# Routed experts: rows gathered for four pairs of experts at a time from two float32r parts, shared down product at the end of the loop

## The reference

```python
x = layer_norm(DEEPNORM_ALPHA * x + mix, ln1_g[l], ln1_b[l])
top_idx, top_w = route(xf, w_router, router_bias)          # 8 of 64 experts for a token
y = routed_experts(xf, top_idx, top_w, w_gate, w_up, w_down) + swiglu(xf, ws_gate, ws_up, ws_down)
x = layer_norm(DEEPNORM_ALPHA * x + y, ln2_g[l], ln2_b[l])

def swiglu(x, wg, wu, wd):
    return (jax.nn.silu(x @ wg) * (x @ wu)) @ wd            # wg, wu: 1024 x 256, wd: 256 x 1024
```

## Time and profile before

| | us |
|---|---|
| median of 3 runs | 1208.05 |
| lowest, highest | 1207.52, 1208.32 |
| the profiled execution | 1209.04 |
| its span, first to last instruction | 1207.1 |

### The profile page before, as it was taken

The page is one execution under the profiler, slowest core; times in us unless marked ns, Lnnn a source line. Parts: engine busy times, 40 slices in busy tenths (PEclk is TensorE's granted clock), DMA queues, the critical chain, the costliest instruction groups (busy, mean ns, idle before and its releaser), DMA issues.

```text
span 1207.1 us, 17937 instructions
## 1 busy us (share of the span) xinstructions
PE 1175.1 (97%) x7776; PEld 552.7 (46%) x7776; DVE 347.1 (29%) x1057; ACT 262.2 (22%) x513; POOL 10.4 (1%) x20
## 2 busy tenths in 40 slices
PE   7999999999999999999899999999999999999994
PEld 6774544444444444343386655344444444444331
DVE  0434712222222222222243345222222222222224
ACT  1132312212222122221112323122212222122210
POOL 0000000000000000000000000000000000000001
PEclk9999999999999999999999999999999999999998
DMA  9973579999999999999997626799999999999993
GB/s 385 423 301 116 212 301 428 428 426 427 427 426 428 428 426 428 428 427 426 422 397 307 235 100 232 329 427 428 426 426 428 426 427 429 424 427 428 426 428 128
DMA packets 36070, 452.41 MB, mean 375 GB/s; under 512 B 3984, under 2 KB 4112, under 8 KB 6928
## 3 DMA queue, kind: packets, MB, share of 16 engines
q1 hardware_dynamic: 35984, 451.18, 89.1%
HBM read 450.12 MB, written 1.05 MB: 374 GB/s over the span
## 4 chain that ended last, share of the span: by engine, by line
PE 82%; DMA 13%; DVE 3%; issue 1%; POOL 0%; ACT 0%; POOLq 0%; DVEq 0%
PE bank L635 31%; PE bank L669 15%; DMA slots<-in_w_gu 13%; PE bank L537 7%; PE bank L568 5%; PE bank L812 5%; PE bank L740 5%; PE bank L749 2%; PE bank L652 1%; PE bank L759 1%; PE bank L769 1%; PE bank L591 1%; PE bank L845 1%; PE bank L556 1%; PE bank L695 1%; PE bank L699 1%
## 5 line engine op out<-in xcount | busy, mean ns | idle before, releaser
L669 PE MATMUL bank<-slots,low 128*32 128x512 f32 x2048 | 233.0, 595 | 1.1 <-issue 1.1
L635 PE MATMUL bank<-slots,low 128*64 128x512 f32 x1024 | 227.0, 594 | 4.5 <-DMA slots<-in_w_gu 4.5
L635 PE MATMUL bank<-slots,xT 128*64 128x512 f32 x1024 | 226.9, 594 | 1.9 <-DMA slots<-in_w_gu 1.9
L1275 DVE SCALAR_TENSOR_TENSOR yparts<-bank,small,yparts 128x512 fp32r<-128x512 f32 x128 | 96.1, 751 | 271.0 <-ACT yparts L972 271.0
L972 ACT ACTIVATE yparts<-bank,small 128x512 fp32r<-128x512 f32 x128 | 88.0, 688 | 255.6 <-PE bank L669 255.6
L635 PEld LDWEIGHTS bank<-slots,low 128*64 128x64 f32 x1024 | 69.1, 137 | 135.2 <-issue 126.3
L635 PEld LDWEIGHTS bank<-slots,xT 128*64 128x64 f32 x1024 | 68.9, 137 | 132.5 <-issue 127.0
L669 PEld LDWEIGHTS bank<-slots,low 128*32 128x32 f32 x2048 | 60.4, 109 | 138.8 <-issue 138.8
L1267 DVE TENSOR_TENSOR high<-high,bank 128x256 f32<-128x256 f32 x64 | 27.0, 421 | 331.7 <-ACT high L1000 331.7
L537 PEld LDWEIGHTS bank<-high,low 128*128 128x128 bf16 x1536 | 100.0, 147 | 48.7 <-issue 48.7
L1000 ACT ACTIVATE high<-bank 128x256 f32<-128x256 f32 x64 | 24.7, 386 | 417.4 <-PE bank L635 417.4
(11 more groups left out here) (125 smaller groups left out, 662.1 us busy)
## 6 DMA issues: line engine op xcount, KB each, us to landing
slots<-in_w_gu SPq DMA_DIRECT2D x128, 2048.0 KB, 24.6
slots<-in_w_dn SPq DMA_DIRECT2D x64, 2048.0 KB, 24.1
slots<-in_dense SPq DMA_DIRECT2D x30, 1024.0 KB, 15.0
slots<-in_first SPq DMA_DIRECT2D x4, 768.0 KB, 7.9
r<-in_pool_mat SPq DMA_DIRECT2D x2, 1024.0 KB, 24.3
r<-in_ln_g SPq DMA_DIRECT2D x4, 512.0 KB, 4.4
r<-in_ln_b SPq DMA_DIRECT2D x4, 512.0 KB, 5.8
sdn<-in_shared_dn SPq DMA_DIRECT2D x2, 1024.0 KB, 9.7
```

Source lines behind the costliest of these rows:

```text
L635: m = pe.matmul(H[64 * a:64 * a + 64, :], xg[B % 2][:, k, j, a, :], GU[g][:, a, :, k, :], start=k == 0, stop=k == KD - 1)
L669: m = pe.matmul(Y[half][r0:r0 + 32, :], hT[:, kc * P + 64 * a + 32 * t:kc * P + 64 * a + 32 * t + 32], DN[g][:, a, kc, half * 512:(half + ...
L1275: dve.scalar_tensor_tensor(ysp[:, 1, half * 512:(half + 1) * 512], Y[half][:, :], wslot[:, b:b + 1], ysp[:, 0, half * 512:(half + 1) * 512 ...
```

## The change

- x is split into two float32r parts, the rounded x and what is left (`split`, `split_low`), in place of three bf16 parts.
- A block is four pairs (`SPAN = 4`, 256 places). `gather` fills one bank with one channel group k for four pairs: two tiles by two parts, four matmuls of 256 columns. For block 0 it uses banks of which `FIRST_BANKS` says the order.
- The gathered rows have one buffer, 32 cells over the places of `xT` and what follows it. A pair's 8 cells (one for each k) are those that the same pair of the next block's turn writes again, so a gather goes into cells that were just used; `cell` permutes the numbers from block to block.
- `sel` stands once in float32r (for gathering, one buffer) and once in bf16 (`selb`, two buffers, for `turn_sel`). DVE builds both.
- `shared_down` moves from pair 0 to behind pairs 27 to 30, a quarter each, and adds to the accumulators; the first `combine`, in pair 1, starts them. `shared_turn` of tile 1 moves from ahead of pair 0 into it.
- Space: `hT`, `w3` and `selb` now stand in `r8`, so norm 2's rows go into slot 1, when pair 31 is done with its first half. At the end of layer 0 SP waits for pair 31's H ahead of memory and chunk 0, and norm 2's rows come between their halves.

```diff
+SPAN = 4
+BLOCKS = PAIRS // SPAN
+FIRST_BANKS = (4, 5, 6, 7, 2, 1, 6, 7)
...
-            def norms(l, g_, b_):
-                sp.dma_start(lng, g_.rearrange("l (o d) -> l o d", o=1)[l].to_broadcast([P, D])).then_inc(ln_in, 16)
-                sp.dma_start(lnb, b_.rearrange("l (o d) -> l o d", o=1)[l].to_broadcast([P, D])).then_inc(ln_in, 16)
+            def norms(l, i):
+                for to, w in ((lng[i], (ln1_g, ln2_g)[i]), (lnb[i], (ln1_b, ln2_b)[i])):
+                    sp.dma_start(to, w.rearrange("l (o d) -> l o d", o=1)[l].to_broadcast([P, D])).then_inc(ln_in, 16)
+
+            def last_norms(l):
+
+                sp.wait_ge(main.h_half, (l + 1) * PAIRS)
+                norms(l, 1)
...
                 if l:
-                    sp.wait_ge(main.h_full, last + 1)
+                    sp.wait_ge(main.h_full, l * PAIRS)
...
                     sp.dma_start(r[:, a:z], dense[l, 0][:, a:z]).then_inc(chunk_in[0][h], 16)
+                    if h == 0:
+                        last_norms(l - 1)
...
-                sp.wait_ge(*x_at(l, 0, NT - 1))
-                norms(l, ln2_g, ln2_b)
...
+            def gather(ps, k, to):
+
+                for t in range(NT):
+                    for s in range(2):
+                        m = pe.matmul(to[:].rearrange("p (x t c) -> p x t c", x=2 * SPAN, t=NT)[:, :, t, :],
+                                      xsp[:, t, s, k::KD], sel[:, t, :].rearrange("p (x c) -> p x c", x=2 * SPAN),
+                                      start=s == 0, stop=s == 1)
                 m.then_inc(ps.g_full, 1)
...
+                if round_ is None:
+                    pe.wait_ge(split_rd, 2 * l + 2)
                 pe.wait_ge(ps.sel_rd, first_block + 1)
-                for t in range(NT):
+                for k in range(KD):
                     if round_ is None:
-                        pe.wait_ge(split_rd, 2 * l + t + 1)
-                    for f in range(4):
-                        if round_ is None and t == 0 and f == 2:
+                        to = bank[FIRST_BANKS[k]]
+                        if k == 2:
                             pe.wait_ge(*read_at(l, "shT0"))
-                        for kk in range(2):
-                            m = gather_rows(kk, t, f, 0, bank[4 + f])
-                        if t == NT - 1:
-                            m.then_inc(ps.g_full, 1)
+                        if k >= 6:
+                            pe.wait_ge(ps.g_sb, first_fill + k - 3)
...
+                    gather(ps, k, to)
                 if round_ is None:
-                    shared_turn(l, 1)
                     pe.wait_ge(w3_rd, l + 1)
...
                     for k in range(KD):
-                        if q == 0 and k in (4, 6):
-                            pe.wait_ge(ps.g_sb, first_fill + k // 2 + 1)
+                        if q == 0:
+                            pe.wait_ge(ps.g_sb, first_fill + max(k + 1, 2 if round_ is None else 6))
...
-                            gather(ps, 2 * j + i, (B + 1) % 2, Y[i])
+                            gather(ps, 2 * j + i, Y[i])
...
                     if first and round_ is None:
-                        for i in range(4):
-                            shared_down(l, i // 2, i % 2)
+                        shared_turn(l, 1)
...
                         turn_sel(ps, q + 1)
+                        if round_ is None and q >= PAIRS - 5:
+                            i = q - (PAIRS - 5)
+                            shared_down(l, i // 2, i % 2)
...
+                for k in range(KD):
+                    g_out(0, k, bank[FIRST_BANKS[k] if round_ is None else 4 + k % 4])
...
-            def split_last(l, t):
-                dve.wait_ge(split_hi, 4 * l + 2 * t + 2)
-                dve.tensor_tensor(xsp[:, t, 2, :], xres[:, t, :], xsp[:, t, 1, :], ALU.subtract).then_inc(split_rd, 1)
+            def split_low(l, t):
+                dve.wait_ge(split_hi, 2 * l + t + 1)
+                dve.tensor_tensor(xsp[:, t, 1, :], xs[:, t, :], xsp[:, t, 0, :].bitcast(F32), ALU.subtract).then_inc(split_rd, 1)
...
+                    for to, done in ((sel, ps.sel_rd), (selb[:, B % 2], ps.selb_rd)):
...
-                    if q % 2 == 0 and q // 2 + 1 < BLOCKS:
+                    if q % SPAN == 0 and q // SPAN + 1 < BLOCKS:
+                        dve.wait_ge(ps.g_full, KD * (turn * BLOCKS + q // SPAN + 1))
```

More of the change, by code:

```diff
@@ L165, in build @@
         xs = sb("xs", [P, NT, D])
-        xT = sb("xT", [P, KD, S])
         cst = sb("cst", [P, NCONST])
+        with nc.sbuf_tensor("selr", [P, NT * SPAN * 64], F32R) as selr:
+            pass
         r8 = sb("r8", [P, 2048])
@@ L173, in build @@
         power = sb("power", [P, 1])
-        low = sb("low", [P, YS_AT])
+        with nc.sbuf_tensor("cells_at", [P, 2 * KD * S], F32), nc.sbuf_tensor("xparts", [P, NT * 2 * D], F32R) as xparts:
+            pass
+        front = sb("front", [P, KD * S + YS_AT])
+        xT = front[:, 0:KD * S].rearrange("p (k s) -> p k s", k=KD)
+        low = front[:, KD * S:]
         with nc.sbuf_tensor("yparts", [P, 2 * D + 2 * P], F32R) as yparts:
@@ L204, in build @@
         rt = pT[:, 0, :]
-        memT = xT[:]
+        memT = xT
         def prob_of(c):
@@ L236, in build @@
         top = part(NT * 8)
-        shared_hT = part(2 * F)
+        shared_hT = sw[:, 0:2 * F]
         assert off[0] <= YS_AT + 2 * D
@@ L240, in build, with cell, cells_of @@
         sdn = sb("sdn", [P, KF * D])
-        xg = [v.rearrange("p (k r e s) -> p k r e s", k=KD, r=2, e=2)
-              for v in (xT[:].rearrange("p k s -> p (k s)"), xg_odd)]
+        cells = front[:, 0:2 * KD * S].rearrange("p (c e s) -> p c e s", e=2, s=64)
+        def cell(B, k, j):
+            return sum(1 << (b + 2 * B) % 5 for b in range(5) if SPAN * k + j >> b & 1)
+        def cells_of(B, k):
+            v = front[:, 0:2 * KD * S].rearrange("p (a b c d e w) -> p a b c d e w", a=2, b=2, c=2, d=2, e=2)
+            at, r = cell(B, k, 0), 2 * B % 5
+            ix = [slice(None) if b in (r, (r + 1) % 5) else at >> b & 1 for b in range(4, -1, -1)]
+            return v[(slice(None), *ix, slice(None))], r == 4
         GU = [slots[:, i, 0:2 * W_CHUNK].rearrange("p (k e j n) -> p e j k n", e=2, j=2, k=KD) for i in range(3)]
@@ L561, in turn_sel, with combine @@
                 m.then_inc(ps.selT_ps, 1)
-            def combine(ps, n, b, half):
+            def combine(ps, n, b, half, begins=None):
                 pe.wait_ge(ps.lo_rd, 2 * n + half + 1)
+                if begins is not None:
+                    for t in range(NT):
+                        fill(begins, f"acc{2 * t + half}")
                 for s in range(2):
@@ L569, in combine @@
                                       ysp[64 * t:64 * t + 64, s, half * 512:(half + 1) * 512],
-                                      start=False, stop=False, skip_group_check=True)
+                                      start=begins is not None and s == 0, stop=False, skip_group_check=True)
                 if half:
@@ L654, in body @@
                     if not first:
+                        begins = l if q == 1 and round_ is None else None
                         if filling:
-                            combine(ps, n - 1, 1 - b, 0)
-                        combine(ps, n - 1, 1 - b, 1)
+                            combine(ps, n - 1, 1 - b, 0, begins)
+                        combine(ps, n - 1, 1 - b, 1, begins)
                     pe.wait_ge(ps.w_in[2][g], (turn * USES[g] + use) * 16 + 16)
@@ L1000, in body @@
                     act.activation(sg[:, 0, :], H[:, 0:F], ACT.Silu).then_inc(ps.silu_rd, 1)
-                    if q // 2 + 1 < BLOCKS:
-                        for f in range(2):
-                            g_quarter(q // 2 + 1, 2 * (q % 2) + f, Y[f])
+                    B, j = q // SPAN, q % SPAN
+                    if B + 1 < BLOCKS:
+                        for i in range(2):
+                            g_out(B + 1, 2 * j + i, Y[i])
+                    if first and round_ is None:
+                        shared_turned(l, 1)
                     act.wait_ge(ps.selT_sb, n + 1)
@@ L1418, in _ @@
                 choose(0)
[L1419 removed]
+                split_low(l, 1)
                 choose(1)
```

120 lines of the change are left out of this document (52 added, 68 removed).

## The result

The changed kernel takes **1240.51 us** (median of 4 runs, 1239.95 to 1241.37) beside 1207.78 for the kernel before on the same chip (1207.47 to 1208.32). The ratio is 1.027, 95% interval [1.0254, 1.0287]: slower by 32.7 us, where 1200.9 had been forecast and 1206.5 was the upper end. The profiled execution took 1241.37 with a span of 1239.4; the span of before is 1207.1, so the traces differ by 32.3 us.

The account below looks back on a forecast made before the run. The DMA's weight stream, by its start and holes, was taken to bound the loops. From 1208.05: -12.1 (hole) + 2.2 (quarters) + 2.7 (between layers) = -7.2, giving 1200.9 us, range 1197.0 to 1206.5.

Parts of the forecast that it names:

- Part 1: First gather and start of pair 0: 32 float32r matmuls at 0.12 us (0.11 to 0.143), 3.84 us, H begins at 150.48.
- rival B: Gather: a float32r matmul of 256 columns costs 0.22 us or its load doesn't hide; 1208.8 us, no change; chance 0.10.
- The end of a loop is set by the stream, not by PE's time for a pair: Expert loops: the weight stream's start and holes set the end; a pair's weights take 14.7 us, PE 13.74.
- the hole: Gap of 6.7 us per layer in the weight stream, because pair 0's down matmuls release their slot late.
- part 3: Loop end: shared-product quarters of 1.73 us behind pairs 27 to 30 cost 1.1 us per layer, +2.2 (0.5 to 1.6 each).
- PE's work of a pair: Later pairs: PE falls from 13.74 to 13.07 us, a gain of 0.6 us x 56 pairs, called worth nothing.
- the two thresholds: Prices of a gathering matmul: the loop turns to PE's pace from 0.31 us; the sum is already zero near 0.21.
- Part 2: Start of each loop: the hole in the weight stream closes, data 6.05 us earlier per layer, 12.1 in all.
- Part 4: Between the layers: late memory, chunk 0 and norm rows make PE stand 2.7 us in L709 (1.6 to 3.2).
- Rival D: Clock falls while PE stands in L709; the 24 matmuls left cost 5.2 us more, 1206.1 us; chance 0.06.

Follow-up runs that it names:

- e1: Changed kernel with x's parts stored channel group by channel group, gather weights at step 1 instead of 8 floats, splits reading with the step: 1208.18 us, ratio 1.0005.
- after: The changed kernel itself, as measured and profiled: 1240.51 us beside 1207.78 for the kernel before.
- e2: Kernel before, bf16 gathers kept, with only the shared down product moved, in quarters behind pairs 20 to 23: 1201.14 us, ratio 0.9949.
- e5: Changed kernel with weights at step 1, written in channel order, norm rows last, quarters behind pairs 20 to 23: 1201.47 to 1201.84, once 1216.52; again 1201.2 us.
- e8: e5 with the quarters of the shared product behind pairs 27 to 30, as in the changed kernel: 1202.86 us.
- e9: Changed kernel with gather weights at a step of 2 floats, norm rows last and quarters behind pairs 20 to 23: 1198.71 us, ratio 0.993.
- e6: e2 with its three bf16 parts stored channel group by channel group, weights at step 1 instead of 8: 1236.48 us, ratio 1.0243.
- e10: Changed kernel with the gathering matmuls reading the same cells as plain f32 instead of float32r: 1368.64 us, one execution.
- e3: Changed kernel with the second norm's rows loaded behind both halves of memory and chunk 0: 1235.6 us, ratio 1.023.

## Why the prediction was wrong, step by step

- **Part 1, the price of a gathering matmul: this step failed, and it decides the result.** 0.12 us was taken, with 0.143 as the upper bound; it is 0.242. None of the three rows that stood for it has four-byte weights at this step in a plain matmul: L537's are bf16, 16 bytes apart, L568's lie side by side, and L920's loads, which do have the step, belong to transposes and are for a reason still open not slowed. L709, the row against rival B, has its weights side by side too. The number itself is right for weights at step 1 or 2 (0.119 in e1). Of the 32.3 us, the first gathers give about 9 (from the gather's first record to H 8.0 us in each layer, 3.4 before), and the loops' 16.9 are of the same cause: with the price mended, in e1, they are 12.8 and 13.6 us shorter than after's. The Trainium skill (SBUF — State Buffer, "Specifications (TRN2)") says that the memory has lines of 16 bytes and wants at least two hits in a line for full bandwidth. The loads at steps 8, 4, 2 and 1 agree with it, L920's do not; the prediction weighed the page on the load's length and not this one.
- **"The end of a loop is set by the stream, not by PE's time for a pair": this step failed as well.** Two sums compete in a loop. PE's, without its waits, was 450.1 - 3.2 = 446.9 us; the stream's was 450.1 with the hole and, by the prediction's own count, 594.9 - 150.5 = 444.4 without. The longer one counts. (The 444.4 holds the 1.1 us that part 3 put on the quarters.) Closing the hole alone could give only 3.2 us per layer and not 6.05 (e2 shows it), and PE's work of a pair, declared worth nothing, was worth everything beyond those 3.2. At the forecast's 0.12 the stream's sum is the longer one again (e1, e5, e8 and e9 all wait for `in_w_gu`), so this step alone would not have moved the forecast. It decides what the wrong price costs: rival B, which kept this step, put 0.22 at 1208.8, and 1240.5 was measured. After the change PE's sum is 458.6. That a pair of 14.20 us is still below 14.7 misled: three pairs are loaded ahead, and the difference of 0.5 us a pair doesn't use them up in 32 pairs (PE never waits for weights in after).
- **Rival B had the price (0.22) and the wrong time** (1208.8), since it kept the stream as the pace. So did the two thresholds. From after's 458.6 with some 28 x 8 = 224 matmuls in the loop, PE's sum falls to 444.4 at 0.242 - 14.2/224 = 0.18 us a matmul: an estimate from these rows, and the point that the prediction put at 0.31.
- **Part 2, the hole: right in size, cause and that it closes.** The windows show it, in after at 369 and in e2 at 431 GB/s. Where the price is mended, the loop comes out nearly as counted: 444.4 forecast, 445.80 and 445.06 in e1, 443.88 and 446.16 in e8. The forecast as a whole does not: e1, the change with the price alone mended, takes 1208.18 and lies outside the range. Its trace is 1.6 us longer than before's where -7.2 was summed, and 5.1 of these 8.8 us lie between the layers (+7.8 against +2.7).
- **Part 3, the quarters at the end:** 2.2 us forecast; e8 against e5 gives 1.1 by the medians, within the scatter. In after itself PE never waits in the loop, so it has no slack for them, and they should count in full there, in one place as in another; that was not run.
- **Part 4, the wait between the layers: right in kind, too small.** 2.7 us (1.6 to 3.2) forecast, 3.87 measured. SP issues as forecast (start, us, line), the norm rows (L447) between the halves:

```profile
605.19 0.33 SPq L485 DMA_DIRECT2D front<-in_memt  x1
...
606.04 0.43 SPq L447 DMA_DIRECT2D slots<-in_ln_g  x1
606.51 0.65 SPq L447 DMA_DIRECT2D slots<-in_ln_b  x1
...
607.98 0.46 SPq L487 DMA_DIRECT2D slots<-in_dense  x1
```

  The second half of chunk 0 is there at 618.9, 13.7 us after H, where 12.4 was summed; from 606 to 608 the DMA moves 217 GB/s, half the rate of the sum.
- **Rival D came true in part.** It was given 0.06 because PE had run for 400 us until just before. The clock fell to 0.50 all the same after 3.9 us of idle time, and came back within 4 us: 1.7 us instead of the 5.2 of a fall over all 24 matmuls (2.9 in e1, after 4.7 us of idle time). The Trainium skill (TensorE: Matmul & The Clock Gate, "Part 1: The HAM clock gate") says that an idle PE is put back to its low level; the windows 620 to 624 agree, and long work ahead was no protection.

Put together: with the step mended, the norm rows last and the quarters at pairs 20 to 23 the change gives 1198.7 (e9) to 1201.8 (e5), where the forecast for the change itself was 1200.9. That it lands there is luck and no proof of the forecast: 2.7 us of wait and 2.2 us for the quarters, which the forecast held, are gone from it.

## What to carry to other kernels

Before an instruction is priced from a like one, compare the access pattern of its operands too, the weights' step above all: here 32 bytes between weights doubled a matmul's cost, and two neighbouring floats were enough to undo it. In a loop where the chain changes from one engine to the other, add up both sums and take the longer one: what an engine waits is all that the other side can gain, and work added beyond that wait costs in full. Before the layout is turned for one reader, price the writers: here ACT's split went from 1.06 to 2.06 us when it read four-byte elements at a step of 8 (e1), and to 4.76 when it wrote two-byte elements at a step of 128 (e6).

## What the runs showed of the hardware that was not expected

- Weights at a step of 4 or 8 floats: 328 and 336 ns a load, 0.24 us a matmul of 256 columns; at 2 or 1: 195 and 188 ns, 0.12. The same for f32 and float32r (e10), but not for the transposes of L949 (192 ns at step 8). For bf16 at step 8 (16 bytes) a load lasts 147 ns against 98 at step 1, and a matmul of 128 columns 0.068 against 0.060 us (the earlier trace rows and e6).
- An f32 matmul of 256 columns is two records in the trace, 0.49 us in e10; a float32r one is one record.
- A 128 x 1024 split: ACT 1.06 and DVE 1.22 us with both sides in order; 2.06 and 2.01 reading four-byte elements at a step of 8 (e1); 1.99 and 1.97 writing them at a step of 128 (e5); 4.76 and 4.72 writing bf16 at a step of 128 (e6).
- The clock: after 450 us of work a wait of 3.9 us was followed by a stretch at 0.50 (after), and so were waits of 2.8 us in the middle of a loop (e1, e8); after 0.9 us (e3) it stayed at 1.00.
- Loops that PE paces repeat to 0.1 us from run to run (458.62, 458.68, 458.63, 458.69); loops that the DMA paces scatter more: 443.06 to 445.11 in two executions of e5's kernel, 443.06 to 446.17 over e1, e5, e6, e8 and e9.
